# An mLSTM layer inside a two-layer backbone step: values transposed into another PSUM accumulator, a convolution placed inside the gate chain, other work between weight units, and the last head reordered

## The reference, cut to what matters

```
qk, v, o, gates = split(h @ w_in)
qk = silu(dwconv3(qk, conv_w, conv_b));  q, k = split(qk)     # K and Q pass a convolution over 3 tokens
ig, lf = gates, log_sigmoid(gates)                            # input and forget gate, forward and backward
b = cumsum(lf);  intra = b[t] - b[s] + ig[s];  m_row = max(b + m, max(intra))
s = (q k^T) * exp(intra - m_row)                              # masked weights between tokens
num = exp(b + m - m_row) * q C + s v;  den = ...;  h = num / max(|den|, exp(-m_row))
C_new, n_new, m_new = the state of the context tokens
h = h_fwd + h_bwd;  hn = (h - mean) * rsqrt(var + eps) * norm_w
y = (sigmoid(o) * hn) @ w_out
```

## Time and profile before

| what | value |
|---|---|
| median of 3 runs | 2058.8 us (2053.92 to 2059.46) |
| the profiled execution | 2058.55 us |
| its span | 2056.7 us |
| PE busy | 1849.4 us, 90% of the span |
| DVE, ACT, POOL busy | 1157.5, 806.5, 646.0 us |
| mean granted TensorE clock | 0.959 |
| bytes moved | 164.94 MB, 80 GB/s over the span |

### The profile page before, as it was taken

The page is one execution under the profiler, slowest core; times in us unless marked ns, Lnnn a source line. Parts: engine busy times, 40 slices in busy tenths (PEclk is TensorE's granted clock), DMA queues, the critical chain, the costliest instruction groups (busy, mean ns, idle before and its releaser), DMA issues.

```text
span 2056.7 us, 31136 instructions
## 1 busy us (share of the span) xinstructions
PE 1849.4 (90%) x11636; PEld 1694.0 (82%) x11636; DVE 1157.5 (56%) x1640; ACT 806.5 (39%) x1203; POOL 646.0 (31%) x278
## 2 busy tenths in 40 slices
PE   6999999986979999999986889886697999999996
PEld 2348888874979999999986878786587999999995
DVE  6994766664557751577437435433246774167733
ACT  6983545544263321233226434443225332123322
POOL 0002121212555433333444221121255443333342
PEclk9999999997989999999998999997898999999998
DMA  9981111110112222222210111110021222222221
GB/s 385 365 335 59 48 47 50 47 48 1 62 41 72 71 80 74 65 77 76 85 59 26 47 46 52 36 57 26 0 82 42 72 71 85 62 68 73 80 82 51
DMA packets 49054, 164.94 MB, mean 80 GB/s; under 512 B 5584, under 2 KB 11216, under 8 KB 48848
## 3 DMA queue, kind: packets, MB, share of 16 engines
q1 hardware_dynamic: 42640, 159.68, 23.2%
q10 hardware_dynamic: 6336, 4.20, 0.7%
HBM read 159.12 MB, written 4.74 MB: 80 GB/s over the span
## 4 chain that ended last, share of the span: by engine, by line
PE 74%; DVE 9%; ACT 7%; issue 3%; DVEq 3%; DMA 2%; POOL 1%; ACTq 0%; SPq 0%; POOLq 0%
PE pj L511 63%; DMA awr<-in_w_ada 2%; PE mO L875 2%; PE psO L676 2%; DVE alo L1526 2%; PE psS L634 2%; PE psT L650 1%; DVE X L1609 1%; ACT h32t L1022 1%; PE psT L659 1%; DVE pr L1707 1%; DVEq L1608 1%; ACT ahi L1102 1%; PE mT L900 1%; ACT whi L1007 1%
## 5 line engine op out<-in xcount | busy, mean ns | idle before, releaser
L408 POOL TENSOR_TENSOR wlo<-wraw,whi 128x1024 fp32r<-128x1024 f32 (+1 forms) x132 | 357.1, 2706 | 999.1 <-ACT whi L1007 999.1
L511 PE MATMUL pj<-Hh,whi 128*128 128x322 f32 x2432 | 588.5, 324 | 81.6 <-POOL Hl L428 27.7
L511 PE MATMUL pj<-Hl,whi 128*128 128x322 f32 x2432 | 569.8, 316 | 0.0
L511 PE MATMUL pj<-Hh,wlo 128*128 128x322 f32 x2432 | 566.0, 314 | 0.0
L511 PEld LDWEIGHTS pj<-Hh,whi 128*128 128x128 f32 x2432 | 415.1, 193 | 103.2 <-issue 66.0
L511 PEld LDWEIGHTS pj<-Hl,whi 128*128 128x128 f32 x2432 | 420.3, 193 | 0.0
L511 PEld LDWEIGHTS pj<-Hh,wlo 128*128 128x128 f32 x2432 | 420.1, 193 | 0.0
L1007 ACT CAST whi<-wraw 128x1024 fp32r<-128x1024 f32 (+1 forms) x184 | 203.9, 1108 | 302.2 <-PE pj L511 299.3
L1577 DVE SCALAR_TENSOR_TENSOR X<-pj,mods,X 128x129 f32<-128x129 f32 (+1 forms) x144 | 54.7, 436 | 284.9 <-PE pj L511 284.8
L1632 DVE SCALAR_TENSOR_TENSOR fcv<-fus,vec,fcv 128x644 f32<-128x644 f32 x88 | 174.4, 1982 | 15.1 <-issue 15.1
L1630 DVE SCALAR_TENSOR_TENSOR fcv<-fus,vec,fcv 128x644 f32<-128x644 f32 x88 | 164.3, 1867 | 15.2 <-issue 15.2
(11 more groups left out here) (298 smaller groups left out, 2373.7 us busy)
## 6 DMA issues: line engine op xcount, KB each, us to landing
awr<-in_w_ada SPq DMA_DIRECT2D x96, 512.0 KB, 5.7
wraw<-in_w_up SPq DMA_DIRECT2D x88, 512.0 KB, 3.6
wraw<-in_w_dn SPq DMA_DIRECT2D x32, 704.0 KB, 4.0
wraw<-in_w_qkv SPq DMA_DIRECT2D x24, 512.0 KB, 3.6
wraw<-in_w_mlin SPq DMA_DIRECT2D x24, 512.0 KB, 3.6
wraw<-in_w_wo SPq DMA_DIRECT2D x8, 512.0 KB, 3.5
wraw<-in_w_mlout SPq DMA_DIRECT2D x8, 512.0 KB, 3.6
X<-in_xT SPq DMA_DIRECT2D x1, 2576.0 KB, 15.8
```

What stands on the lines that cost most here:

```text
L408: nc.gpsimd.tensor_tensor(wlo[k][:, 0:width], wraw[k][:, 0:width], whi[k][:, 0:width].bitcast(F32), ALU.subtract).then_inc(w_lo, 1)
L511: last = mm(out[:, c, 0:HALF], w, x[:, j, c * HALF:(c + 1) * HALF], start=(j == 0 and n == 0), stop=(j == n_k - 1 and n == 2))
```

## The change

- `m_turn_v` transposes the values into `mO` rather than into `mT`. It waits for `mo_free` (v0) and for the new semaphore `mv_lo` (v1), and the values leave the list of `mT` users.
- In head 0, v0 and v1 are copied into `hOt` (a view of `hO`) rather than into `h32`, so v0's copy no longer waits for `mk_ready`.
- `m_conv(0, 1)` moves into `gate_rows`, right behind `a_ready`. `gate_exps` moves ahead of head 0's list on ACT.
- On PE scores 3 with turn 2, and scores 4 with turn 3, now stand between two units. `rows(h + 1, 0)` stands between o1 and the next head's v0. `m_turn_v` of head h >= 1 stands behind 3 and behind 8 k-steps of the early unit.
- On ACT the sigmoid of o moves from in front of `m_c_hi` to behind `m_turned(h, 1)`. `mevac("o0")` moves ahead of `m_q_hi`.
- In the last head ACT casts `O32m` rows 0 and 1 before `m_exps(h, 4)`. The sigmoid goes behind `m_turned(h, 4)`. On PE `values 1` goes ahead of the first `out` pieces, and `m_mean` directly behind `values 2`.

```diff
 def _ml_uses():
-    order = []
+    order = [("a", 0), ("a", 1), ("g", 0)]
     for h in range(ML_HEADS):
+        if h:
+            order += [("a", 2 * h + 1), ("t", 5 * h - 1)]
+        order += [("k", h), ("t", 5 * h)]
         if h:
             order.append(("c", h - 1))
+        order.append(("t", 5 * h + 1))
         if h:
             order.append(("s", h - 1))
         order += [("n", h), ("t", 5 * h + 2), ("t", 5 * h + 3)]
+        if h + 1 < ML_HEADS:
+            order.append(("a", 2 * h + 2))
...
             def m_turn_v(h, w):
                 pe.wait_ge(pj_copied, MCOP + _ml_unit(f"v{w}", h) + 1)
-                m_wait(("v", 2 * h + w))
+                if w:
+                    pe.wait_ge(mv_lo, 2 * h + 1)
+                elif h > 0:
+                    pe.wait_ge(mo_free, 3 * h)
+                v = (h32 if h else hOt)[w]
...
-                    last = nc.tensor.transpose(flatT[:, c * P:(c + 1) * P], h32[w][:, col:col + P], ident[:, :])
-                last.then_inc(mt_full, 1)
+                    last = nc.tensor.transpose(flatO[:, c * P:(c + 1) * P], v[:, col:col + P], ident[:, :])
+                last.then_inc(mv_full, 1)
...
# PE, head h >= 1 (after)
+                    unit("v0", h, range(0, 5))
+                    rows(h, 1)
+                    unit("v0", h, range(5, 8))
+                    m_scores(h, 0)
+                    m_turn(h - 1, 4)
+                    unit("v1", h, range(0, 3))
+                    m_turn_k(h)
+                    unit("v1", h, range(3, 8))
+                    m_values(h - 1, 2)
+                    m_scores(h, 1)
+                    m_turn(h, 0)
+                    early(0, range(0, 3))
+                    m_turn_v(h, 0)
+                    m_mean(h - 1)
+                    early(0, range(3, 8))
+                    m_turn_v(h, 1)
# PE, head 0 (after)
+                    unit("v1", h, range(0, 4))
+                    rows(h, 1)
+                    unit("v1", h, range(4, 8))
+                    m_turn_v(h, 0)
+                    gate_tables()
+                    m_scores(h, 0)
+                    early(0, range(0, 2))
+                    m_turn_k(h)
+                    early(0, range(2, 4))
+                    m_turn_v(h, 1)
+                    m_scores(h, 1)
+                    m_turn(h, 0)
+                    early(0, range(4, 8))
# PE, every head (after)
                 m_scores(h, 2)
                 m_turn(h, 1)
+                early(1, range(0, 3))
                 if prev:
                     m_square_sum(h - 1)
                 m_values(h, 0)
+                early(1, range(3, 5))
                 m_states(h)
+                early(1, range(5, 8))
                 m_scores(h, 3)
                 m_turn(h, 2)
# last head (after)
+                    m_values(h, 1)
                     out(0, range(0, 2))
+                    m_scores(h, 4)
+                    m_turn(h, 3)
+                    out(0, range(2, 6))
                     m_turn(h, 4)
+                    out(1, range(0, 2))
                     m_values(h, 2)
                     m_mean(h)
+                    out(1, range(2, 6))
                     m_square_sum(h)
# other heads (after)
+                    unit("o0", h, range(0, 4))
+                    m_values(h, 1)
+                    unit("o0", h, range(4, 8))
+                    m_scores(h, 4)
+                    m_turn(h, 3)
                     unit("o1", h, FULL)
+                    rows(h + 1, 0)
```

More of the change, by code:

```diff
@@ L259, in hybrid_step @@
             sig = sb("sig", [P, 2, TP], F32, s)
+            hOt = [hO[:, k, :] for k in range(2)]
             gr = [O32m[0:GR, k, :] for k in range(6)]
@@ L858, in m_values @@
             def m_values(h, part):
-                use = ("v", 2 * h + 1) if part == 0 else ("t", 5 * h + 2 * part)
-                pe.wait_ge(mt_free, MUSE[use] + 1)
+                pe.wait_ge(mt_free, MUSE["t", 5 * h + 2 * part] + 1)
+                if part == 0:
+                    pe.wait_ge(mv_lo, 2 * h + 2)
                 if part == 1:
@@ L1414, in m_head @@
                     m_out(h - 1, 2)
+                    m_c_hi(h)
+                    m_turned(h, 0)
+                    m_exps(h, 2)
+                    m_v_hi(h, 0)
+                    m_squares(h - 1)
+                    early(0)
+                    m_v_hi(h, 1)
+                    m_turned(h, 1)
                     m_sigmoid(sig[:, :, :])
+                    m_rstd(h - 1)
                 else:
[L1417 to L1418 removed]
+                    mevac("v0", h, hOt[0])
                     m_ab(h, 0)
                     m_ab(h, 1)
[L1421 removed]
+                    mevac("v1", h, hOt[1])
+                    m_v_hi(h, 0)
                     m_exps(h, 0)
[L1423 to L1424 removed]
+                    m_v_hi(h, 1)
                     m_exps(h, 1)
[L1426 to L1436, removed]
+                    m_turned(h, 0)
+                    m_c_hi(h)
+                    m_exps(h, 2)
+                    early(0)
+                    m_turned(h, 1)
                 m_exps(h, 3)
                 m_states(h)
+                early(1)
                 m_turned(h, 2)
[L1440 removed]
                 m_out(h, 0)
[L1442 removed]
                 if last:
[L1444 removed]
                     act.wait_ge(tile_done, U_MLOUT)
                     output_hi(O32m, mout_done, range(0, 2), per=2)
+                    m_exps(h, 4)
+                    output_hi(O32m, mout_done, range(2, 4), per=2)
                     m_out(h, 1)
[L1448 removed]
+                    output_hi(O32m, mout_done, range(4, 6), per=2)
                     m_turned(h, 3)
                     m_turned(h, 4)
+                    m_sigmoid(h32t[:, :, :])
                     m_out(h, 2)
@@ L1488, in _ @@
             m_k_hi(0)
+            gate_exps()
             for h in range(ML_HEADS):
@@ L2012, in m_head @@
                 m_mask(h, 1)
[L2013 to L2017, removed]
                 if prev:
                     m_turned(h - 1, 4)
-                m_weights(h)
-                m_c_lo(h)
-                m_turned(h, 0)
-                m_combine(h, 1)
-                m_v_lo(h, 0)
-                if prev:
-                    m_centre(h - 1)
-                m_v_lo(h, 1)
+                    m_combine(h, 0)
+                    m_weights(h)
+                    m_c_lo(h)
+                    m_turned(h, 0)
+                    m_combine(h, 1)
+                    m_v_lo(h, 0)
+                    m_centre(h - 1)
+                    m_v_lo(h, 1)
+                else:
+                    m_v_lo(h, 0)
+                    gate_tables()
+                    m_combine(h, 0)
+                    m_weights(h)
+                    m_v_lo(h, 1)
+                    m_turned(h, 0)
+                    m_combine(h, 1)
+                    m_c_lo(h)
                 m_turned(h, 1)
```

66 lines of the change are left out of this document (14 added, 52 removed).

## The result

| | before | after |
|---|---|---|
| median | 2058.2 us (4 runs) | 1998.1 us (1995.3 to 1999.0, 4 runs) |
| ratio | 1 | 0.9708 (95%: 0.9697 to 0.9719) |
| profiled execution, span | 2058.55, 2056.7 | 1995.32, 1993.4 |

A forecast was written before the change was run, and what follows sets the result against it. PE's own instruction stream, busy 90% of the span, was taken as the limit. Gains of 6 (head 0), 19.6 (middle heads), 10.8 and 22.3 (last head) sum to 58.7, from 2058.55 to 2000 us; range 1988 to 2023.

The forecast's parts named there:

- Middle heads: Heads 1 and 2: each falls to 73.5 us, from 83.8 and 82.8, together a gain of 19.6.
- the six units at 42.8: Middle head: its six units take 42.8 us of PE's 67.4 at full speed, each 7.13 to its successor's start.
- The new wait at turn(h-1, 4): Behind scores 0: PE newly waits about 2.7 us for the mask, plus 1.5 for slow clock.
- What goes: Middle heads: waits for mVl and behind the values vanish, and all three bare unit boundaries are filled (two by 1.6, 1.3).
- Head 0: First head: gains 6 us, of which 4 around v0's copy, starting 2.0 earlier; bounds 2 to 10.
- of the other waits 4 to 5 remain: First head: of its other waits, 7.3 us and seven times 0.3, about 4 to 5 remain in other places.
- Last head up to turn 2: Last head's first part: turn 2 ends at 51.3 us with slow clock, against 62.1, a gain of 10.8.
- Tail: Last head after turn 2: the 12.6 wait for Hl goes; 42 us against 64.3, a gain of 22.3.
- Rival 1: Heads 1 to 3 ahead of turn 2: waits return at hand-overs, half the 30.4 gain lost, 2015 us; chance 0.17.
- rival 4: Whole change: mT waits weren't the limit, others of the same length stood behind them; 2056 us; chance 0.02.
- Rival 2: Last head's end: it keeps its stall, from late Hl or bare turn 4 and mean; 2022 us; chance 0.07.
- rival 3: Clock doesn't recover between short waits: mild 2014 us, chance 0.07; strong, a whole head at half speed, 2067, chance 0.03.

The follow-up runs named there:

- ab_first: Changed kernel with the gate row's copy m_ab(h, 1) ahead of v0's copy and split on ACT in heads 1 to 3; 1991.0 us, ratio 0.9668.
- v_in_ring: Changed kernel with the values back in mT and in its list, in the new order of all engines; 2033.4 us, ratio 0.9879.
- sigmoid_old: Changed kernel with the sigmoid of o back in front of m_c_hi on ACT; 2011.2 us, ratio 0.9769.
- bare_bounds: Changed kernel with nothing between o0 and o1, nor between o1 and v0, in heads 0 to 2; 2006.2 us, ratio 0.9743.
- tail_act_old: Changed kernel with only ACT's list of the last head's end in its old order, PE's new order kept; 2006.2 us, ratio 0.9755.
- gate_old: Changed kernel with K's convolution behind the gate chain and gate_exps behind head 0's ab copies, as before; 2002.3 us, ratio 0.9720.
- last_turn2: Changed kernel with the last head's scores 3 and turn 2 ahead of o1's last three k-steps; 1997.4 us, ratio 0.9706.
- tail_old: Changed kernel with the last head's end in its old order on both PE and ACT; 2021.4 us, ratio 0.9818.
- v0_first: Changed kernel with head 0's v0 copy and first gate row's copy ahead of gate_exps on ACT; 1995.0 us, ratio 0.9688.

## Why the prediction was right, point by point

The total of 2000 against 1998 is closer than its terms: in each of the four stretches errors of 1 to 3 us cancel in part, which is luck. The mechanisms are right where it says so below.

- **Middle heads: forecast 73.5, measured 74.55 and 73.3. The sum is right, its terms less so.** I took 67.4 for PE's work at full speed; ab_first shows 69.3. I then added three small waits of 0.5, 0.7 and 0.7 for ACT's copy of the early unit, for `turned 1` and for o0's copy. None exists, in the change or in ab_first. That fits a PE that arrives later than in my walk at places where 0.5 to 0.7 were missing: ab_first reaches early1 at t = 35.0, where 36.5 less the wait of 2.7 gives 33.8. So the two errors are probably one, seen from both sides. The term that was mis-sized is the six units at 42.8. Start to start, head 1 of ab_first has 44.8 for their pieces (0.2 of it the one wait), 9.5 for the values, 4.3 for the scores and 10.9 for the rest, which I had taken as 11. Its o1, which nothing interrupts, shows why:

```profile
1249.07 0.54 PE L511 MATMUL pj<-Hh,whi 128*128 128x322 f32 x2
...
1256.41 1.12 PE L812 MATMUL mT<-Ar,ident 4*128 4x512 f32 x2
```

That is 7.34 until the next piece starts, and not 7.13. The subtracted overlap holds between two matmuls of line 511, but the units are cut into twelve pieces with other work between them, and each pays about 0.15 (1.8 over 12).
- **The new wait at turn(h-1, 4): forecast 2.7, measured 2.83, three times.** The mechanism (ring, `ab` behind v0's copy and split) is shown by ab_first, which removes it by that swap alone. For the slow clock behind it I had put 1.5; it cost 2.7, 1.4 and 0 in the three heads (last section).
- **What goes.** No wait for `mVl` or `mApl`, none at the boundaries. v_in_ring, sigmoid_old and bare_bounds each bring their own back.
- **Head 0: forecast 6, measured 6.7, or 8.0 on equal work.** PE's wait for v0's copy fell by 2.3, as said (2.0). Of the waits behind it the trace has 0.62, 0.83 and 0.17, 1.6 in all, where I had put 4 to 5. So the term "of the other waits 4 to 5 remain" was about 3 too large: o0's copy of 1.6 didn't appear, and early0's of 1.9 was 0.17; nor did DVE's stretched combine 3 beside POOL set anything. And the sum leaves out that head 0 takes over the next head's gate row, 1.3. The two partly cancel.
- **Last head up to turn 2: forecast 10.8, measured 12.0. Tail: 22.3 against 21.8.** The first is over by the slow clock that I had added and that this execution doesn't have (1.00). The tail's waits were 1.9 (forecast 2.0), 2.7 for `out` 2 to 5 (1.7), 1.33 (1.2), 0.7 (0.8), and 7.49 (7.5). The 3 that I had added for slow clock is not there: from 1379.3 to 1413.8, up to the square sum, the granted clock is 1.00. Without it the forecast is 39.1 against the measured 42.5. One of the 3.4 is the wait of `out` 2 to 5; the rest I can't put down to a line, but unit pieces priced too low would show in this way.
- **Rivals.** Rival 1 (waits return at the hand-overs) and rival 4 fall by the list of waits. Rival 2 falls; tail_act_old shows that a late `Hl` alone would have brought 8 to 10 of its 22. The strong form of rival 3 falls. Its mild form is seen in part: the clock did fall, but behind the long waits (6.6 and 7.5) and two of the three of 2.8. Over the 5 us from the end of the waits of 0.62, 0.83 and 1.88 it is 1.00.

## What to carry to other kernels

When several transposes share one PSUM buffer in a fixed order, look at what each release waits for. A user with long steps on two other engines (here the values) is worth another buffer, and even more so once the order around it is rewritten; the two edits must be priced together (here 16 to 18 and 25 alone, 60 as one). Before a wait is blamed on the slowest producer, look for ready work behind it on the waiting engine: `values 1` stood there. And after each reordering read the new list of waits for one whose producer is queued behind something unrelated, as `ab` behind a copy and a split: that swap was the cheapest gain of the study.

## What the runs showed of the hardware that was not expected

**The same wait, three clocks.** In the kernel after, PE waits 2.83 at the same instruction in heads 1, 2 and 3. The 5 us behind it:

```profile
1193.30:1198.30 5.00, 4.97 (x20) 5.00 (x21) 2.20 (x10) 1.49 (x3) 1.08 (x1) 0.50 0.36 108
1267.90:1272.90 5.00, 5.00 (x26) 5.00 (x27) 2.23 (x10) 1.46 (x3) 1.05 (x1) 0.68 0.33 105
1341.20:1346.20 5.00, 5.00 (x36) 4.99 (x37) 2.92 (x12) 1.83 (x5) 1.02 (x1) 1.00 0.35 105
```

Half speed throughout, partly, and not at all. What that costs can be read directly, as the time from the turn behind the wait to `m_turn_k`, with three k-steps in between. Head 1 and head 3:

```profile
1193.33 1.51 PE L844 MATMUL mT<-ident,mA 128*128 128x128 f32 x6 [2.83 <-DVE am L1911]
...
1199.44 0.27 PE L861 MATMUL mT<-ident,h32t 128*128 128x128 f32 x1
...
1341.17 0.85 PE L844 MATMUL mT<-ident,mA 128*128 128x128 f32 x6 [2.83 <-DVE am L1911]
...
1344.56 0.27 PE L861 MATMUL mT<-ident,h32t 128*128 128x128 f32 x1
```

That is 6.1 against 3.4 us: 2.7 lost in head 1, 1.4 in head 2 (4.8 us), nothing in head 3. The 1.25 between the middle heads' lengths is of this size. The same wait stands in nine profiles, 27 times in all: the change, bare_bounds, gate_old, last_turn2, sigmoid_old, tail_act_old, tail_old, v0_first and v_in_ring. Ten times nothing was lost up to `m_turn_k`, fifteen times 1.2 to 1.6, twice 2.7, with no head that always pays. So here a wait of 2.8 cost between its own length and nearly twice that, about 1 more on average, and a single profile of one kernel doesn't tell which.

**Tiny DVE operations held by POOL.** During `Hl` in the last head, first DVE and then POOL:

```profile
1382.27 1.23 DVE L1929 TENSOR_TENSOR mdn<-mdn 128x2 f32<-128x2 f32 x1
1383.57 1.46 DVE L1931 SCALAR_TENSOR_TENSOR mdn<-mdn 128x2 f32<-128x2 f32 x1
...
1394.26 1.31 DVE L1929 TENSOR_TENSOR mdn<-mdn 128x2 f32<-128x2 f32 x1
```

```profile
1381.90 3.11 POOL L428 TENSOR_TENSOR Hl<-O32m,Hh  x2
```

Each takes 0.16 otherwise, on 2 elements per partition. The first of them ends at 1383.50 and the second at 1385.03, and POOL's two pieces, half of 3.11 each, end at about 1383.5 and 1385.0. The Trainium skill, "SBUF — State Buffer", section "SBUF: two separate sides", counts DVE operations with two SBUF inputs among those that the port lock holds against a POOL operation that reads SBUF; these have two, and the trace agrees. Each time a small step of the chain waits for the end of the running POOL instruction, about 2.4 us of combine 3 here, and turn 4's wait of 1.33 stands behind combine 4 with the third row.
